# A fused two-norm sum, engine-made copies for a depthwise convolution, and an in-place weight ring in a one-core transformer kernel

## The reference

```
# block 1: gated linear attention, dilated attention in 4 heads, gates, MLP
x = x + mix
x = x + square(relu(rmsnorm(x, ln2) @ w_mlp1)) @ w_mlp2
x = x + sigmoid(rmsnorm(x, ln3) @ w_pg) * (p @ w_pp)
x = rmsnorm(x, ln_f)                        # end of block 1
# block 2: two layers
h = x
for i in range(2):
    h = h + 0.5 * swiglu_ffn(rmsnorm(h, ffn_norm1[i]), ...)   # takes the norm just above again
    m = rmsnorm(h, mix_norm[i])
    if i == 0:
        u = m @ w_pw1;  a, b = split(u);  u = a * sigmoid(b)
        u = depthwise_conv(u, w_dw)         # causal, 31 taps, each of the 1024 channels by itself
        h = h + silu(rmsnorm(u, g_norm)) @ w_pw2
    else:
        h = h + mla(m, ...)                 # latent attention, 8 heads
    h = h + 0.5 * swiglu_ffn(rmsnorm(h, ffn_norm2[i]), ...)
out = rmsnorm(h, final_norm)
```

## Time and profile before

| | |
|---|---|
| median of 3 runs | 1679.87 us (1679.61 to 1682.29) |
| the profiled execution | 1683.39 us, span in the trace 1681.7 us |
| PE busy | 1575.4 us (94%), mean granted clock 0.963 |
| DVE, ACT, POOL busy | 1053.4, 669.0, 97.7 us |
| DMA | 264.5 MB, mean 157 GB/s |

### The profile page before, as it was taken

One profiled execution on the slowest core, in us unless ns is written; L12 is line 12 of the kernel. 1 busy time (PEld: TensorE's weight loads), 2 busy tenths in 40 slices (PEclk: granted clock), 3 DMA queues, 4 the chain that ended last, 5 costly groups with the idle time before them and its releaser, 6 DMA issues.

```text
span 1681.7 us, 31102 instructions
## 1 busy us (share of the span) xinstructions
PE 1575.4 (94%) x12781; PEld 1531.1 (91%) x12781; DVE 1053.4 (63%) x1310; ACT 669.0 (40%) x790; POOL 97.7 (6%) x98
## 2 busy tenths in 40 slices
PE   4989899899999996999988899999999999999996
PEld 3989899889999996999976699999999998899995
DVE  5663755459885568655662576667665687766553
ACT  3462334434333343443442354335433343454331
POOL 2000000002000015000020000000000000100000
PEclk7998999999999997999999899999999999999997
DMA  4642564335556542664679266546655554365551
GB/s 136 199 136 61 154 189 147 112 121 172 183 178 210 175 146 76 200 188 147 196 177 172 77 183 185 165 154 216 189 180 164 165 164 135 93 184 176 164 184 39
DMA packets 272695, 264.53 MB, mean 157 GB/s; under 512 B 16199, under 2 KB 271541, under 8 KB 272586
## 3 DMA queue, kind: packets, MB, share of 16 engines
q1 hardware_dynamic: 271770, 260.99, 52.3%
q0 software_dynamic: 816, 1.99, 0.4%
HBM read 257.21 MB, written 1.07 MB: 154 GB/s over the span
## 4 chain that ended last, share of the span: by engine, by line
PE 79%; DVE 8%; DMA 5%; issue 3%; ACT 2%; SPq 1%; POOL 1%; POOLq 0%; DVEq 0%; ACTq 0%
PE ps L540 72%; DMA raw<-in_conv_w_pw_dram 2%; PE misc L676 1%; DVE wsplit L1038 1%; DVE xa L1056 1%; PE misc L575 1%; PE misc L565 1%; ACT wsplit L848 1%; SPq L484 1%; PE misc L725 1%; DMA plain<-plain 1%; PE misc L653 1%; DMA raw<-in_mla_w_uq_dram 0%; PE misc L683 0%; POOL acc L1509 0%
## 5 line engine op out<-in xcount | busy, mean ns | idle before, releaser
L540 PE MATMUL ps<-xa,wsplit 128*128 128x256 f32 x7104 | 872.4, 285 | 13.6 <-DVE xa L1056 12.6
L540 PEld LDWEIGHTS ps<-xa,wsplit 128*128 128x128 f32 x7104 | 863.6, 193 | 19.5 <-issue 9.3
L848 ACT CAST wsplit<-raw 128x1024 fp32r<-128x1024 f32 (+2 forms) x532 | 513.8, 970 | 681.5 <-PE ps L540 214.6
L1038 DVE TENSOR_TENSOR wsplit<-raw,wsplit 128x1024 fp32r<-128x1024 f32 (+2 forms) x532 | 591.7, 1147 | 110.8 <-ACT wsplit L848 91.7
L540 PE MATMUL ps<-parts,wsplit 128*128 128x256 f32 x3984 | 487.6, 285 | 9.7 <-DVE parts L1067 8.5
L540 PEld LDWEIGHTS ps<-parts,wsplit 128*128 128x128 f32 x3984 | 485.1, 194 | 11.3 <-issue 7.9
L1136 DVE TENSOR_TENSOR work<-ps,work 128x512 f32<-128x512 f32 x44 | 30.4, 691 | 94.9 <-PE ps L540 94.9
L1119 DVE TENSOR_TENSOR t<-ps,rstd 128x512 f32<-128x512 f32 x48 | 33.2, 691 | 71.6 <-PE ps L540 71.5
L1509 POOL TENSOR_TENSOR acc<-acc,sq 128x512 f32<-128x512 f32 x36 | 53.6, 1490 | 322.2 <-ACT sq L868 321.7
L890 ACT ACTIVATE work<-t 128x512 f32<-128x512 f32 x48 | 30.3, 632 | 105.6 <-DVE t L1119 105.6
L1506 POOL COPY acc<-sq 128x512 f32<-128x512 f32 x14 | 10.8, 773 | 984.0 <-ACT sq L868 984.0
(11 more groups left out here) (198 smaller groups left out, 650.9 us busy)
## 6 DMA issues: line engine op xcount, KB each, us to landing
raw<-in_ffn_w_dram SPq DMA_DIRECT2D x176, 512.0 KB, 4.3
raw<-in_w_in_dram SPq DMA_DIRECT2D x76, 512.0 KB, 4.5
raw<-in_ffn_w_dram SPq DMA_DIRECT2D x96, 384.0 KB, 3.8
raw<-in_w_mlp_dram SPq DMA_DIRECT2D x64, 512.0 KB, 4.5
raw<-in_ffn_w_dram SPq DMA_DIRECT2D x32, 256.0 KB, 3.0
raw<-in_conv_w_pw_dram SPq DMA_DIRECT2D x16, 512.0 KB, 5.2
plain<-plain SPq DMA_DIRECT2D x16, 284.0 KB, 8.7
raw<-in_w_o_gla_dram SPq DMA_DIRECT2D x8, 512.0 KB, 4.3
```

Of the source, the lines that this page charges most:

```text
L540: last = mm(o, still, moves, start=st and n == 0, stop=en and n == 2, skip_group_check=True)
L848: nc.scalar.copy(wsplit[:, slot, 0:kn, 0, 0:p.width], raw[:, s0 % RAW, 0:kn, 0:p.width]).then_inc(hi_done, 1)
L1038: TT(wsplit[:, slot, 0:kn, 1, 0:p.width], raw[:, s0 % RAW, 0:kn, 0:p.width], wsplit[:, slot, 0:kn, 0, 0:p.width].bitcast(F32), ALU.subtrac ...
```

## The change

Three parts:

1. **One scaled sum for two norms.** With y = x*r*g (r the factor of `ln_f`, g its gain), the factor of the next norm times r is 1/sqrt(mean(x*x*(g*g+eps)) + eps*eps). So ACT squares `x` with the scale sqrt(g*g+eps) (`gain_sq`), and one sum gives the factor that `ffn1_up0`'s evacuations need. `w_pp`'s evacuation splits `x` for `ffn1_up0` at once, with the product of both gains (`gain_both`). The plain squares for r are made during groups 0 and 1 of `ffn1_up0`; their sum, root and reciprocal, and the scaling of `x` (`scale_residual`), stand at groups 18 to 21 of `ffn1_up0`.
2. **Convolution copies by engines.** The 16 copies of a pair (32 partitions, 2x256 elements each) are made by ACT (5), DVE (7) and POOL (4) instead of DMAs. The layout puts four channel tiles side by side, so `pw2` is loaded like every other phase, and the taps' layout changes (16 small DMAs instead of 4, two transposes instead of four).
3. **The ring.** `raw` now is the low half of `wsplit[s % 8]` (same addresses). SP loads block s when PE has used block s-8; ACT waits only for the DMA; DVE subtracts in place. ROUND_AHEAD goes from 7 to 5, REST_AHEAD from 5 to 4. In the MLA phase, ACT's root for `cq` moves from behind `mla_kr` to behind group 2 of `mla_a`.

```diff
-RAW = 4
-ROUND_AHEAD = 7
-REST_AHEAD = 5
+ROUND_AHEAD = 5
+REST_AHEAD = 4
+COPIES = [(h, q) for h in range(4) for q in range(4)]
+COPIES_ACT, COPIES_DVE, COPIES_POOL = COPIES[0:5], COPIES[5:12], COPIES[12:16]
...
-        raw = sb("raw", [P, RAW, 4, W])
+        raw_guard = nc.sbuf_tensor("raw", [P, RING, 4, 2, W], F32)
+        raw = raw_guard.__enter__()
+        raw_guard.__exit__(None, None, None)
         wsplit = sb("wsplit", [P, RING, 4, 2, W], F32R)
...
-        add("pw2", cols_of_tiles(a["conv_w_pw2_2"][0]), 4, K8, from_parts(16), ("resid", 1.0, gn["ffn_norm2_2"]))
+        add("pw2", cols(a["conv_w_pw2_2"][0]), 4, K8, from_parts(16), ("resid", 1.0, gn["ffn_norm2_2"]))
...
+        def shift_copy(i, h, q):
+            at = CONV_W - 1 - h
+            return shifted(i)[32 * h:32 * h + 32, :, q, at:at + T], glu[32 * q:32 * q + 32, i % 2, :, :]
...  (SP)
-                if s0 >= RAW:
-                    sp.wait_ge(lo_done, lin(s0 - RAW + 1, RING, i))
+                if s0 >= RING:
+                    sp.wait_ge(used, lin(s0 - RING + 1, RING, i))
...
-                    for h in range(4):
-                        sp.dma_start(shifted(n)[32 * h:32 * h + 32, :, :, :],
-                                     upad[:, n % 2, :, h:h + SHIFTED]).then_inc(s_shift[n % 2], 16)
...  (PE)
-                pe.wait_ge(s_shift[i % 2], SHIFTS * (i // 2 + 1))
+                pe.wait_ge(copied_act, i + 1)
+                pe.wait_ge(copied_dve, i + 1)
+                pe.wait_ge(copied_pool, i + 1)
...
+                        if p.name == "ffn1_up0" and g == 18:
+                            norm_sum_step("ffn1_up0")
...  (ACT)
-                act.wait_ge(raw_landed[s0 % RAW], lin(landed[s0], 16 * RING // RAW, i))
-                if s0 >= RING:
-                    act.wait_ge(used, lin(s0 - RING + 1, RING, i))
-                nc.scalar.copy(wsplit[:, slot, 0:kn, 0, 0:p.width], raw[:, s0 % RAW, 0:kn, 0:p.width]
+                act.wait_ge(raw_landed[slot], lin(landed[s0], 16, i))
+                nc.scalar.copy(wsplit[:, slot, 0:kn, 0, 0:p.width], raw[:, slot, 0:kn, 1, 0:p.width]
...
+            def shift_copies(n):
+                dv_did(act, f"glu{n}")
+                act.wait_ge(pads_zero, 1)
+                if n >= 2:
+                    pe_did(act, f"conv{n - 2}")
+                for h, q in COPIES_ACT:
+                    last = nc.scalar.copy(*shift_copy(n, h, q))
+                last.then_inc(copied_act, 1)
...
+                if name == "ln_f":
+                    for k in range(2):
+                        last = act_fn(sq[:, q % 2, k, :], src[:, k, :], ACT.Square,
+                                      scale=gain_sq[:, 2 * c + k:2 * c + k + 1])
...
+                        if p.name == "ffn1_up0" and g == 18:
+                            norm_step("ffn1_up0")
...
+                        if p.name == "pw1" and g in (2, 4, 6):
+                            shift_copies(g // 2 - 1)
                         evacuate(p, g, None, 0)
-                        if p.name == "mla_kr":
+                        if p.name == "mla_a" and g == 2:
                             norm_step("cq", Q_LORA)
...
+                        if p.name == "ffn1_up0" and g < 2:
+                            for c in (2 * g, 2 * g + 1):
+                                square_pair("ffn1_up0", c, x[:, 2 * c:2 * c + 2, :])
...  (DVE; in the evacuation of a glu group, and of a w_pp group)
+                        for h, q in COPIES_DVE:
+                            ins = vec.tensor_copy(*shift_copy(n, h, q))
+                        ins.then_inc(copied_dve, 1)
...
+                    split_gained(xa[:, 2 * g:2 * g + 2, :, :], xs, 2 * g, 2, gain_both)
...
+                        if p.name == "ffn1_up0" and g >= 18:
+                            if g == 18:
+                                norm_step("ffn1_up0", rstd2)
+                            scale_residual(g - 18)
```

More of the change, by code:

```diff
@@ L51 @@
 BIAS_N = 384
[L52 to L54 removed]
+SHIFTED = T + CONV_W - 1
 COL_HA = 2 * GLA_QK + 2 * GLA_V
@@ L67 @@
 GAIN_N = _n
-SILENT = ("conv", )
+COPIES = [(h, q) for h in range(4) for q in range(4)]
+COPIES_ACT, COPIES_DVE, COPIES_POOL = COPIES[0:5], COPIES[5:12], COPIES[12:16]
+SILENT = ("conv", "ffn1_up0", )
 def bias_table():
@@ L332, in program @@
                    "ffn2_down0": "ffn1_up1", "ffn1_down1": "mla_a", "w_o": "ffn2_up1", "ffn2_down1": "final"}
-        norm_at = {"gla_q": "w_in", "mlp1": "mlp1", "w_pg": "w_pg", "ffn1_up0": "ffn1_up0", "pw1": "pw1",
+        norm_at = {"gla_q": "w_in", "mlp1": "mlp1", "w_pg": "w_pg", "ffn1_up0": "ln_f", "pw1": "pw1",
                    "ffn2_up0": "ffn2_up0", "ffn1_up1": "ffn1_up1", "mla_a": "mla_a", "ffn2_up1": "ffn2_up1",
@@ L798, in _ @@
                     gla_step(5)
-                if p.name == "w_pp":
-                    norm_sum_step("ln_f")
                 if p.name == "pw1":
@@ L874, in norm_step @@
                     act.wait_ge(norm_read, n)
-                last = act_fn(root[:, :], conv_ss if name == "conv" else misc[:, 3, 0:T], ACT.Sqrt, bias=consts[:, 0:1], scale=1.0 / features)
+                last = act_fn(root[:, :], conv_ss if name == "conv" else misc[:, 3, 0:T], ACT.Sqrt, bias=consts[:, 2:3] if name == "ln_f" else consts[:, 0:1], scale=1.0 / features)
                 if token:
@@ L984, in _ @@
                     gla_step(5)
-                if p.name == "w_pp":
-                    norm_step("ln_f")
-                    for c in range(4):
-                        square_pair("ffn1_up0", c, x[:, 2 * c:2 * c + 2, :])
                 if p.name == "pw1":
+                    shift_copies(3)
                     for c in (2, 3):
@@ L994, in _ @@
                         dv_did(act, f"convn{i}")
-                        act.wait_ge(s_gain, 16 * 4)
                         for c in (2 * i, 2 * i + 1):
-                            last = act_fn(plain[:, c, :], plain[:, c, :], ACT.Silu, scale=conv_gain[:, c:c + 1])
+                            at = GAIN_AT["conv_norm_2"] + c
+                            last = act_fn(plain[:, c, :], plain[:, c, :], ACT.Silu, scale=gain[:, at:at + 1])
                         last.then_inc(s_ac, 1)
@@ L1179, in evacuate, with scale_residual @@
                     v.wait_ge(new_x, new_x_at[pair_of[p.name]] + g + 1)
+                    split_gained(xa[:, 2 * g:2 * g + 2, :, :], xs, 2 * g, 2, gain_both)
+            def scale_residual(c):
+                at = GAIN_AT["ln_f"] + 2 * c
+                for k in range(2):
+                    ins = STT(x[:, 2 * c + k, :], x[:, 2 * c + k, :], gain[:, at + k:at + k + 1], rstd2[:, :],
+                              ALU.mult, ALU.mult)
+                done(f"lnf{c}", ins)
             def gla_step(k):
@@ L1373, in _ @@
                     gla_step(5)
-                if p.name == "w_pp":
-                    norm_step("ln_f")
-                    for c in range(4):
-                        xs = x[:, 2 * c:2 * c + 2, :]
-                        step(TT(t2[:, :, :], xs, bcast(rstd[:, :], 2), ALU.mult))
-                        at = GAIN_AT["ln_f"] + 2 * c
-                        TS(x[:, 2 * c, :], t2[:, 0, :], gain[:, at:at + 1], None, ALU.mult)
-                        TS(x[:, 2 * c + 1, :], t2[:, 1, :], gain[:, at + 1:at + 2], None, ALU.mult
-                           ).then_inc(new_x, 1)
-                        v.wait_ge(new_x, new_x_at["ffn1_up0"] + c + 1)
-                        split_gained(xa[:, 2 * c:2 * c + 2, :, :], xs, GAIN_AT["ffn_norm1_2"] + 2 * c, 2)
-                    done("lnf", vec.tensor_copy(stat[:, 6:7], consts[:, 0:1]))
                 if p.name == "pw1":
@@ L1509, in _ @@
                         gp.tensor_tensor(acc[:, :, :], acc[:, :, :], sq[:, q % 2, :, :], ALU.add).then_inc(summed, 1)
+                    if name == "conv" and c < 2:
+                        pl.wait_ge(summed, q + 1)
+                        shift_copies(c + 2)
 TWO_PI = 6.283185307179586
```

123 lines of the change are left out of this document (70 added, 53 removed).

## The result

The changed kernel takes 1633.89 us (median of 4 runs, 1632.81 to 1639.3) beside 1681.08 before: ratio 0.972, 95% interval 0.971 to 0.974, 47 us less. The forecast was 1635.4. The profiled execution of after is the longest of its four, 1639.3 us with a span of 1637.5, so the traces compare 1681.7 with 1637.5: 44.2 us less, where the sum of the terms was 44.5. That the total fits says little, since terms may be wrong in both directions, and a second trace of the same kernel has a span of 1632.6 (49.1 us less). So the span is cut at points that both programs pass, by the start of the PE row named. The last column but one is a second trace of the same changed kernel (experiment e9).

The account below looks back on a forecast made before the run. PE was taken as the bound, busy 1575.4 of 1681.7 us, so gains come from its idle time and low clock. Terms 5.3 + 9.7 + 2.0 + 10.8 + 14.3 + 2.4 = 44.5 gave 1635.4 us, range 1628 to 1652.

Parts of the forecast that it names:

- the start: Sum of squares at the kernel's start: PE takes it near 31.5 instead of 36.84, -5.3 us, bounds 2.4 and 5.4.
- the heads: Attention heads: the transposes' waits in four heads go, -9.7 us; behind them `y_gla`'s first product gains 2.0, bounds 0 and 2.0.
- ln_f: From `w_pp` to `ffn1_up0`: 11.9 us won, second sum costs 1.1, so -10.8 us; bounds -12.5 and -8.
- MLA: The root in MLA moves ahead of two casts that wait for DMAs: -2.4 us, bounds -3 and 0.
- the convolution: Pairs 0 and 3 no longer wait, as the engines' copies hide behind PE's work: -14.3 us, bounds -14.6 and -10.
- the last piece of `x` is there at 27.93 + 0.68: Step of the start's term: `x` is complete at 28.6 us, a square and an addition later it is 30.8.
- Rival (a): The heads keep their wait because the cast is late for another reason: 1647 us; chance 0.12.
- my 644.6: Step of the `ln_f` term: time taken for the end of PE's last six matmuls, from a range of 643.4 to 645.3.
- Rival (b): POOL beside DVE: copies and conv weights slow both, pair 3 waits; gives back 4 to 8 us, about 1641; chance 0.16.
- Rival (c): The shallower ring gives back half a microsecond each at some of 30 phase borders: 1650 us; chance 0.12.
- Rival (d): Slower than before: in-place subtraction takes 2.46 us instead of 1.23, losing 65 us, 1700; chance 0.02.

Follow-up runs that it names:

- e9: The changed kernel once more, unchanged, with more rounds: 1633.7 us, ratio 0.973 to the kernel before.
- e5: The changed kernel with one wait added: at the start ACT squares only once all four pairs of `x` are in SBUF; 1631.3 us.
- e1: The kernel before with only the look-ahead changed (ROUND_AHEAD 7 to 5, REST_AHEAD 5 to 4), old ring kept: 1670.5 us, ratio 0.994.
- e6: The changed kernel with ACT instead of DVE copying `x`'s pairs 1 to 3 out of PSUM: first sum at 32.5 us; total time not given.
- e10: The changed kernel with ACT copying `x`'s pairs 1 to 3, `ha`'s norm ahead of its look-ahead, convolution pair 3 ahead of the sum: 1628.4 us, ratio 0.970.
- e8: The changed kernel with ACT's root for `cq` back behind `mla_kr`: the stage to the rope turns takes 39.36 us; total time not given.
- e2: The kernel before with part 3 alone (ring memory, loads behind `used`, look-ahead), MLA's root not moved: 1663.6 us, ratio 0.990.

## Why the prediction was right, and where it wasn't

The total fits partly by luck. Between before's trace and after's, the start (2.1 us) and the heads (0.9) gave less than forecast; `ln_f` (3.0), MLA (0.8), the convolution (0.3) and the stretch from `pw2` to `mla_a` (2.0) gave more. The stage between gates and scores, which no part touches, took 2.5 us more; in e9's trace it takes 3.2 less. `ln_f` and MLA lie outside their bounds (12.5 and 3).

**Start: -5.3 forecast, -3.2 and -2.3 in the two traces.** The failed step is "the last piece of `x` is there at 27.93 + 0.68". That is a time of before, when POOL was silent. The squares start at 19.96 instead of 29.76, and so POOL works beside DVE's splits. I counted the price of that neighbourhood for DVE's later chain, and forgot it in the arrival of `x`. e5 shows it: POOL silent, `x` at 27.54. It shows as well that there was no 5.3 to be had by that alone, since the additions then come late. Nor were the earlier squares the gain: in e1 they start at 26.4, and its sum comes at 33.8. A second step fails behind it. I took DVE's chain, which frees `ha`'s bank, to end at about 42; it ended at 44.95, 1.4 us earlier than before, since its subtraction behind the splits began 3.3 us later. In after, at a granted clock of 0.70 from 36 to 45 us, PE didn't wait for it; in e6 it waited 2.25. And the row that I read as the split without POOL (1.23) has POOL's copy beside it; without POOL it is 0.88.

**Gates to scores: 0 forecast, +2.5 and -3.2.** Nothing of the change touches it. See the last section.

**Heads and behind: -11.7 forecast, -10.8.** The size is right: 9.7 for the transposes, and `y_gla`'s product took 7.48 where I took 6.1 for granted (1.4 us, inside its bounds of 0 to 2.0, as PE had just waited 2.1 us for a split, 0.5 more than before). In e5, e6 and e10, where the code is the same here, the same product took 5.98 behind the same wait. The rows, from after and then from e5:

```profile
278.45 1.15 PE L570 MATMUL misc<-ident,logit 128*128 128x128 f32 x9
...
337.02 7.48 PE L535 MATMUL ps<-parts,wsplit 128*128 128x256 f32 x48 [2.13 <-DVE parts L1086]
```

```profile
330.29 5.98 PE L535 MATMUL ps<-parts,wsplit 128*128 128x256 f32 x48 [2.13 <-DVE parts L1087]
```

The cause is half right. I wrote that in the new ring the cast only needs its DMA; e1 has the old ring and the same gain. What mattered was which block the cast is of: five ahead is a slot that PE has left. Rival (a) falls.

**ln_f: -10.8 forecast, -13.8.** The evacuations and splits went as worked out (20.0 us to the last six matmuls; my 644.6 stands for 20.6). In figures: 12.5 for the 11.9 forecast, and the second sum costs 1.0 for 1.1. The mis-sized term is the clock, which I had not counted: the first sum of `ffn1_up0` takes 1.03 us instead of 1.90, and PE's granted clock is 1.00 from 631 to 637 us, where before it was 0.58 and 0.56 from 656 to 660, behind a stretch in which PE kept waiting for `xa`; 1.6 together. The remaining 0.7 lie ahead of `w_pp` (0.4) and at `pw1`'s sum (0.3). No stall at group 18, as forecast.

**Convolution: -14.3 forecast, -14.6.** Right in both parts, in after's trace; in e5, e6 and e8, with the same code here, it is -12.9 (last section). DVE's copies took 4.3 us for my 3.0, within the bound of 6.2, and the slack swallowed it. In pair 0 they took 7.54, beyond the bound, beside POOL's tap matrices, and the group that covers them was long enough. Rival (b) was real as a mechanism (1.90 for 0.88, and 4.31 for 2.9) but cost nothing here; it cost 2.3 us of `x`'s arrival at the start, where I had not placed it. By the Trainium skill (GPSIMD Engine Reference, Key points), GpSimd contends with VectorE instructions that read two SBUF inputs or run in a 2-port mode; the low halves, which read `x` and `xa`, agree: 0.88 without POOL, 1.90 beside it.

**MLA root: -2.4 forecast, -3.2.** Near in size by luck, from a wrong cause. e8 takes the move away and loses nothing. In before the root stood behind casts of blocks seven ahead; e1 (look-ahead) brings 1.1 us of it and e2 (the ring) the other 2.1.

**Nothing forecast, -2.0 found, from `pw2` to `mla_a`:** 0.8 in `pw2`'s first product at a better clock, 1.2 at two borders, where PE waited for `xa` before. Rival (c) had the sign wrong for the ring, which gave at borders. The shorter look-ahead without it did cost at one: in e1 PE waits twice for `xa` (0.37 + 0.45) ahead of `ffn1_up1`'s sum, once before (0.44), and that stage is 0.6 us longer. Rival (d) falls with the subtraction's 1142 ns. The last stage is 0.7 us longer, all in the DMA of the output.

## What to carry to other kernels

Work that moves into a stretch where another engine was idle changes the durations of everything beside it: take them from a row in which the neighbour was busy, for each step of the chain and not only the last. A look-ahead number and the memory behind it are one decision; a cast seven ahead was late in the old ring and ruinous in the new one, and two constants alone gave 10.7 us of the 17.6 that look like the ring's. When PE waits for a sum, see whether anything behind it in PE's program could go first: two exchanged lines gave 3.4 us.
